# A Mamba-2 and attention trunk on one core: in the scan, the products of the states with C are put one projection later

## The reference, cut to what matters

```python
proj = h @ w_in                       # z, x, B, C, dt
xbc = silu(depthwise_conv5(xbc) + conv_b)
# each direction, chunks of 128 positions, 8 groups of 4 heads:
y_diag = einsum('bclgn,bcsgn,bgrcls,bcsgrp->bclgrp', C, B, L, X)
states = einsum('bcsgn,bgrcs,bcsgrp->bcgrpn', B, decay_states, X)
# prev: the running state ahead of each chunk
y_off = einsum('bclgn,bcgrpn,bgrcl->bclgrp', C, prev, exp(a_cs))
y = y_diag + y_off                    # both directions summed
y = y + xs * d_skip
y = rmsnorm(y * silu(z), norm_w) @ w_out
```

## Time and profile before

| what | us |
|---|---|
| median of 3 runs | 789.28 |
| lowest and highest run | 786.24, 794.48 |
| the profiled execution's own time | 788.04 |
| its span in the trace | 786.2 |

### The profile page before, as it was taken

How to read it: one execution, slowest core, us unless ns; L and a number is a source line. 1 busy time by engine, 2 the same in 40 slices (tenths; PEclk the granted TensorE clock), 3 DMA queues, 4 the chain that set the end, 5 groups by cost and what they waited for, 6 DMA issues and landing times.

```text
span 786.2 us, 11647 instructions
## 1 busy us (share of the span) xinstructions
PE 759.6 (97%) x3868; PEld 614.0 (78%) x3868; DVE 485.9 (62%) x888; ACT 408.0 (52%) x814; POOL 450.1 (57%) x259
## 2 busy tenths in 40 slices
PE   6999999999999999998999999999999999999897
PEld 5778888888878788887888887877777777777575
DVE  3778868585868768695941111475666666666554
ACT  6556563738274554737532244356455564555440
POOL 6455684948484866748844334774555555455150
PEclk9999999999999999999999999999999999999899
DMA  9274555654626455443623224313222133121002
GB/s 263 57 247 113 184 138 161 150 173 102 185 81 151 152 140 181 134 162 105 217 86 110 82 80 131 104 54 104 80 80 78 54 104 102 55 83 48 0 1 108
DMA packets 100197, 91.11 MB, mean 116 GB/s; under 512 B 5456, under 2 KB 87728, under 8 KB 97080
## 3 DMA queue, kind: packets, MB, share of 16 engines
q1 hardware_dynamic: 95760, 66.99, 29.0%
q10 hardware_dynamic: 4264, 23.50, 9.9%
q0 software_dynamic: 128, 0.05, 0.0%
HBM read 88.13 MB, written 2.39 MB: 115 GB/s over the span
## 4 chain that ended last, share of the span: by engine, by line
PE 72%; DVE 16%; issue 4%; ACT 4%; POOL 2%; DMA 1%; DVEq 0%; ACTq 0%; POOLq 0%; SPq 0%
PE bank L1389 61%; DVE c_acc L1028 6%; PE bank L1518 2%; PE bank L1618 2%; PE bank L1492 1%; PE bank L1504 1%; DVE tmp L1079 1%; ACT c_acc L686 1%; PE bank L1648 1%; PE bank L1466 1%; ACT w_hi L641 1%; DMA rows<-in_x 1%; DVE rows L1055 1%; PE bank L1479 1%; POOL h L606 1%
## 5 line engine op out<-in xcount | busy, mean ns | idle before, releaser
L500 POOL TENSOR_TENSOR w_lo<-w_raw,w_hi 128x1024 fp32r<-128x1024 f32 x104 | 258.6, 2489 | 241.1 <-ACT w_hi L641 240.9
L1389 PE MATMUL bank<-hn_hi,w_hi 128*128 128x512 f32 x384 | 154.3, 402 | 4.4 <-DVE BT L1043 3.8
L1389 PE MATMUL bank<-hn_hi,w_lo 128*128 128x512 f32 x384 | 150.1, 391 | 0.0
L1389 PE MATMUL bank<-hn_lo,w_hi 128*128 128x512 f32 x384 | 149.6, 390 | 0.0
L641 ACT CAST w_hi<-w_raw 128x1024 fp32r<-128x1024 f32 x104 | 108.1, 1043 | 70.8 <-PE bank L1389 66.0
L1389 PE MATMUL bank<-w_hi,hn_hi 128*128 128x512 f32 x320 | 128.4, 401 | 3.3 <-DVE hn_lo L1143 2.5
L1389 PE MATMUL bank<-w_hi,hn_lo 128*128 128x512 f32 x320 | 125.1, 391 | 0.0
L1389 PE MATMUL bank<-w_lo,hn_hi 128*128 128x512 f32 x320 | 124.6, 389 | 0.0
L1028 DVE SCALAR_TENSOR_TENSOR c_acc<-bank,par,c_acc 128x510 f32<-128x510 f32 (+1 forms) x128 | 95.9, 749 | 26.1 <-ACT c_acc L686 16.9
L1389 PEld LDWEIGHTS bank<-hn_hi,w_hi 128*128 128x128 f32 x384 | 72.2, 188 | 22.2 <-issue 6.5
L1389 PEld LDWEIGHTS bank<-hn_hi,w_lo 128*128 128x128 f32 x384 | 72.1, 188 | 15.6
(11 more groups left out here) (206 smaller groups left out, 1263.6 us busy)
## 6 DMA issues: line engine op xcount, KB each, us to landing
w_raw<-in_ssd_w_in SPq DMA_DIRECT2D x48, 512.0 KB, 4.1
w_raw<-in_attn_w_in SPq DMA_DIRECT2D x64, 256.0 KB, 3.1
rows<-acs_rows ACTq DMA_DIRECT2D x14, 1024.0 KB, 6.6
edec<-exp_rows ACTq DMA_DIRECT2D x16, 512.0 KB, 6.5
w_raw<-in_ssd_w_out SPq DMA_DIRECT2D x16, 512.0 KB, 3.5
w_raw<-in_attn_w_out SPq DMA_DIRECT2D x16, 256.0 KB, 3.1
wbias<-bias_rows SPq DMA_DIRECT2D x8, 448.0 KB, 4.1
rows<-in_x SPq DMA_DIRECT2D x4, 512.0 KB, 5.2
```

Source lines behind the costliest of these rows:

```text
L500: nc.gpsimd.tensor_tensor(w_lo[:, s, :], w_raw[:, s, :], f32(w_hi[:, s, :]), ALU.subtract)\
L1389: ins = T.matmul(dst, a[i], b[j], start=first and n == 0, stop=last and n == 2)
```

## The change

TensorE does the off products of groups g0 to g6 in slot 4, behind B's projection, instead of slot 3, behind x1's. On DVE `within 1` stays in slot 3; the four `from`, three of the `add` and `gated 0` go behind B's silu, and `add 3` goes to slot 5, between C's conv and `gated 1`. So DVE's order is then

- slot 3: conv x1, within 0, silu x1, within 1;
- slot 4: conv B, silu B, from 0, from 1, add 0, add 1, from 2, from 3, gated 0, add 2;
- slot 5: conv C, add 3, gated 1, silu C.

No instruction is added or removed, and no DMA is touched. g7 is as it was.

```diff
                 if slot == 3 and not last_g:
+                    within(g, 1, half)
+                if slot == 4 and not last_g:
                     from_states(g, 0, tmp)
                     from_states(g, 1, c_tan)
                     add_states(g, 0, tmp)
...
                     gated(g, 0)
-                    within(g, 1, half)
-                if slot == 4 and not last_g:
-                    add_states(g, 3, c_tan)
+                    add_states(g, 2, tmp)
...
-                    if scan and slot == 4 and slot in slots:
-                        add_states(m * 2 + half, 2, tmp)
                     if scan and slot == 5 and slot in slots:
+                        add_states(m * 2 + half, 3, c_tan)
                         gated(m * 2 + half, 1)
...
-                if slot == 3 or slot == 4 and last_g:
+                if slot == 4 or slot == 3 and last_g:
...
-                        if slot == 4:
+                        if slot == 4 and last_g:
                             pe.wait_ge(off_used, g * 4 + n - 1)
```

## The result

The changed kernel takes **795.25 us** (median of 20 runs, 791.52 to 799.52) against 789.14 (20 runs, 785.12 to 794.48): 6.1 us more by the medians, and 5.8 by the **ratio of 1.0074 (interval 1.0054 to 1.0094)**. Forecast were +5.8 us and 794.

What follows compares the result with a forecast made beforehand. TensorE, busy 759.6 of 786.2 us, was taken as the bound. New waits 5.4 + 5.8 plus fills 0.7, less old waits 6.1, gave +5.8 us, so 794 us (chance 0.48), range 785 to 800.

Steps and rivals of the forecast that it cites:

- The stall aimed at: Start of the next slot 0: TensorE's waits for B's silu, 4.9 us late in all, gone everywhere.
- Part 2: DVE from slot 4's end to slot 1': TensorE waits for C's silu, 5.4 us in all.
- Part 3: Start of slot 4: TensorE waits for x0's silu, 5.8 us in all; bounds 1.7 and some 8.
- the race: Slot 2: DVE's second `tmp <- prev, dec2` against POOL's split; later squares lose it in all four loop groups, 4 x 1.0 us.
- The fills: TensorE: one more change between small and 512-column matmuls per group, 7 x 0.1 = 0.7 us.
- g0: First group's slot 4: start waits for x0's silu, 1.45 us.
- old waits, gone: Scan: the old waits for B's silu and of off for the running states go, less 6.1 us in all.
- a loop group longer by 0.9 to 1.5: Sign in the changed profile: each of g2 to g5 longer by 0.9 to 1.5 us.
- A: Rival: only the wait at slot 1' comes, the race at slot 4 is not lost; +1.7, 789.7 us; chance 0.22.
- B: Rival: faster, C's silu in time because the conv of C begins 1.15 us earlier; 784.3 us; chance 0.1.
- C: Rival: worse, ACT late everywhere, B's evacuation waits, more waits in slots 2' and 3'; 798.5 us; chance 0.15.
- D: Rival: nothing changes, the waits sum to the same; 788 to 789 us; chance 0.05.

Runs made afterwards that it cites:

- e3: VectorE's order as in the changed kernel, TensorE's as in the kernel before (off behind x1's projection); 819.33 us, ratio 1.0358 to the kernel before.
- e1: Changed kernel with GpSimd's additions of squares one slot later, behind the split of slot 3; 792.43 us, ratio 1.0021 to the kernel before.
- e9: e4 with GpSimd's squares one slot later; 787.22 us, ratio 0.9969 to the kernel before.
- e2: Kernel before, with only GpSimd's squares moved one slot later; 787.43 us, ratio 0.9963 to the kernel before.
- e5: Changed kernel with g0 in the old order on both engines, only g1 to g6 changed; 794.86 us, ratio 1.0059 to the kernel before.
- e10: The kernel of e7 measured once more, beside e8; 779.84 us, ratio 0.9887 to the kernel before.
- e7: e6 with GpSimd's squares one slot later; 781.51 us, ratio 0.9891 to the kernel before.
- e4: Changed kernel with C's silu ahead of gated 1 in slot 5; 805.87 us, ratio 1.0177 to the kernel before.
- e6: Changed kernel, but the first two off products and their dependents stay in slot 3, gated 1 behind C's silu; 793.95 us, ratio 1.0039 to the kernel before.
- e8: e7 with gated 1 ahead of C's silu again; 786.03 us, ratio 0.9968 to the kernel before.

## Why the prediction was right, point by point

**The stall aimed at.** Forecast: gone in all groups. Measured: gone in all groups, the 0.3 us still listed being ahead of the scan. (So the seven waits of the earlier trace rows were not one in each of g0 to g6 but that one and six; g1's was too short to be listed.) e3 shows that the earlier end of slot 4 did this, not VectorE's order.

**Part 2, slot 1'.** Forecast: DVE needs 15.65 us from slot 4's end, TensorE 14.5, so waits of 1.1 in the loop and 0.33 in written-out groups, 5.4 in all. The mechanism held, and the loop's term was too small. Slot 1' stands behind the transposes, and without a wait it begins 0.79 us behind their start. In the changed kernel, g1 and g2 (slot 4's end in g2 is the start of off at 175.41):

```profile
145.27 1.04 PE L1465 MATMUL bank<-ident,xT 128*128 128x128 f32 x8
146.35 0.50 PE L1388 MATMUL bank<-hn_hi,w_hi 128*128 128x512 f32 x1
...
175.41 2.84 PE L1517 MATMUL bank<-CTr,prev 128*128 128x128 f32 x24
188.99 1.04 PE L1465 MATMUL bank<-ident,xT 128*128 128x128 f32 x8
191.34 0.47 PE L1388 MATMUL bank<-hn_hi,w_hi 128*128 128x512 f32 x1 [1.31 <-DVE CTr L1043]
```

From start to start the waits are 1.45 to 1.56 us in g2 to g5, 0.25 more than the idle times of 1.20 to 1.31, since the row of the transposes reaches beyond the place where slot 1' could begin. In g0, g1 and g6 slot 1' begins 1.18, 1.08 and 1.17 behind the transposes: waits of 0.3 to 0.4 that no list names, as forecast. In all that is 7.2 us where I had 5.4. In g2 VectorE's chain took 15.93 us (175.41 to 191.34), 0.3 more than forecast: two additions followed by an instruction that needs their end cost 0.79 and 0.72 (185.04 to 185.83, 189.18 to 189.90) where I had put 0.6 for each. TensorE needs 14.4, 0.1 less.

**Part 3, slot 4.** Forecast: all four loop groups lose the race, 1.0 each. Measured: lost in all four, idle times of 0.96 to 1.03, and slot 4 begins 1.0 to 1.1 later than the 1.90 us behind diag's start that it has in e1. The second products take 2.37 to 2.41 us and not the 2.9 forecast, because they begin 0.5 behind the split and not 0.04; they end 0.5 behind its end either way. In g1 slot 4 is 0.6 late and in g6 0.7, against 0.3 and 0.1: there the first product was held up by 0.9 us and the race was lost as well. e1 turns the race off and gives 4.1 us back in the loop groups. The reason given (squares late by 0.5 us through ACT) held: gated 1 ended at 190.59, 0.75 us ahead of slot 1' (forecast 0.8, before 1.4), and the exps behind it began at 190.77, 0.6 ahead against 1.2 before.

**The fills.** Forecast 0.7 us for seven more changes between small and 512-column matmuls. The runs show no such price: a group in TensorE's changed order without a wait takes 42.39 us (e9, g1), and g2 of the kernel before without its wait takes 43.26 - 0.78 = 42.48.

**g0.** Forecast 1.45 at slot 4. In the profiled execution it was 4.08, and then the granted clock was 0.50, the 1.2 GHz level, for the stretch that follows:

```profile
82.00:85.00 3.00, 3.00 (x9) 2.32 (x8) 2.88 (x5) 1.33 (x2) 0.00 (x0) 0.50 0.86 237
85.00:90.00 5.00, 5.00 (x30) 4.35 (x29) 0.98 (x2) 1.10 (x2) 2.40 (x1) 0.96 0.97 394
```

This is not in the forecast. By the starts g0 lost 4.15 us at slot 4, 2.3 by the clock behind it and 0.4 at slot 1', less the 1.2 that it had lost before. What made the wait 4.08 and not 1.6 (e1) is not the change but the first masks of g0 on VectorE (L1055, two inputs in SBUF again). In the kernel before (first fence) and in the changed one:

```profile
52.56 4.57 DVE L1055 TENSOR_TENSOR rows<-rows,below 128x1024 f32<-128x1024 f32 x2
52.97 3.08 POOL L500 TENSOR_TENSOR w_lo<-w_raw,w_hi 128x1024 fp32r<-128x1024 f32 x1 [3.02 <-ACT w_hi L641]
```

```profile
53.80 5.19 DVE L1055 TENSOR_TENSOR rows<-rows,below 128x1024 f32<-128x1024 f32 x2 [1.01 <-DMA rows<-acs_rows]
53.11 2.38 POOL L500 TENSOR_TENSOR w_lo<-w_raw,w_hi 128x1024 fp32r<-128x1024 f32 x1 [3.02 <-ACT w_hi L641]
```

It is the same kind of race, and here the landing of a DMA seems to decide it. Over the twelve profiles g0's second product begins 1.2 to 1.4 us behind the start of diag in five (before, e1, e2, e5, e10) and 3.8 to 3.9 behind it in seven, under old orders of TensorE (e3) as under new ones. In the five the masks begin 0.2 to 0.4 us ahead of the split, and the first two take 4.6; in the seven they begin 0.01 to 0.7 behind it and take 5.2 to 5.9, and in six of these the profile names the DMA as what they waited for (in e3 nothing). e3, with the old order, waits for the second product at off, 3.40 us. That this also spreads the runs of each kernel over some 8 us is likely, but only argued: no run moved the masks or the DMA. In an execution where the masks were early, e1's, g0 waits 1.63 at slot 4, and its step is 44.46 against 43.62: 0.8 us for the change in g0, forecast 0.7.

**The sum.** Forecast +5.8, measured +5.8 by the ratio and +6.1 by the medians. The size of each part was less exact. For g1 to g6, counted by starts (a group without a wait takes 42.40):

| us, g1 to g6 | forecast | measured |
|---|---|---|
| new waits at slot 1' | 5.1 | 6.8 |
| new waits at slot 4 | 4.4 | 5.6 |
| fills | 0.6 | 0 |
| old waits, gone | -5.0 | -5.4 |
| change of the steps | 5.1 | 6.65 |

The measured parts add up to 7.0, 0.3 more than the steps; I can't place that. With 0.8 for g0 the scan is 7.5 us longer, not 5.8, and that lies at the edge of the interval (4.3 to 7.4). What lies outside differs the other way: behind g7's diag the changed kernel's profile has 403.7 us and the one before 405.6. But this stretch varies from 403.7 to 406.1 over the twelve profiles, and by as much between e7 and e10, which are one kernel (405.9, 403.8), so it is not the change's. The place and the kind of each loss were forecast; that the total agrees to some tenths is in part luck, a sum of errors of both signs within the noise of the runs. Of the signs named, "a loop group longer by 0.9 to 1.5" was missed twice (1.68 in g2 and g5).

**The rivals.** A (the race is not lost, +1.7) has its picture in e1, +2.6 us by the medians and +1.7 by the ratio. B (faster) falls: C's silu was late. Its point was right, though: e7 shortens what stands ahead of the conv of C, and gains. C (worse everywhere, 798.5): its mechanism, ACT too late for an evacuation, came true in e4, not here; in the changed kernel x0's evacuation at 159.16 follows the projection's end by 0.4 us, and B's at 175.76 follows slot 4's end by 0.35, behind a split of ACT that ended 0.5 before. D (no change) falls: the interval excludes it.

## What to carry to other kernels

Where three engines hand a unit around, a stall that is moved away from one operand shows up at the next one whose chain has less slack than the move gives it: add up the second-latest chain before moving anything. An instruction of VectorE with two inputs in SBUF next to one of GpSimd is a race of 0.1 us with a price of 2 us; look at which starts first, and move the one with the most slack (here the squares: behind the split of slot 2, where they now run, GpSimd stood idle for 7.6 us) away from it. One such move was worth 3 to 4 us in the changed kernel, 1 to 3 in the kernel before, and by the ratios 12 in e6 and 16 in e4. Last, idle times in a list are shorter than the delays: sum them from start to start.

## What the runs showed of the hardware that I had not expected

TensorE's granted clock fell behind single waits of 2.2 to 4.1 us inside dense work, to 0.50, the 1.2 GHz level; over a longer stretch the view shows a mean of the two levels. It fell behind 4.08 us (the changed kernel, g0), behind 3.1 (e3, g2: means of 0.74 and 0.63), behind 2.44 (e3, g1: 0.72 over 6 us) and behind 2.23 and 2.17 (e4, g4 and g5: 0.69 and 0.68). It did not behind 2.15 us in g3 of the same e4. And the length of the wait alone does not decide: in g0 it fell to 0.50 behind 3.34 us in e7 and not at all behind 3.35 in e6 and 3.37 in e8. Those three give a price, too: g0's step is 48.71 us in e7 and 45.80 and 45.83 in e6 and e8, so the fall cost 2.9 us. In e3 and e4 it cost 1.6 to 1.7 each. So waits of 2.2 us and more can have a second price, and a sum of waits alone was too small there, as mine were for e3 and e4.
